# Inverse roots as exp(-0.5 ln) on ScalarE, and other places for the adaLN additions, in a two-layer diffusion step

## What is computed

```python
def rmsnorm(x, g):
    y = xf * lax.rsqrt(jnp.mean(xf * xf, axis=-1, keepdims=True) + NORM_EPS)
    return (y * g).astype(x.dtype)

def modulation(cvec, w, b):                     # adaLN: six vectors of 1024 for each layer
    m = jax.nn.silu(cvec) @ w + b
    return jnp.split(m, 6, axis=-1)

# in each layer l, for each token group:
mix = token_mixer(rmsnorm(x, norm1_g[l]) * (1 + sc1) + sh1, ...)
x = x + gt1 * mix
x = x + gt2 * expert_choice_ffn(rmsnorm(x, norm2_g[l]) * (1 + sc2) + sh2, ...)

# in token_mixer: queries and keys of the 8 attention heads are normed one head at a time
nq = head_rms(na_heads(nq), na_q_g)
nk = head_rms(na_heads(nk), na_k_g)
```

## Time and profile before

| | |
|---|---|
| runs of the kernel before | 3173.14, 3174.12, 3202.10 us (median 3174.12) |
| the profiled execution | 3180.14 us, span of its instructions 3178.4 us |
| granted TensorE clock, mean of the span | 0.956 of 2.4 GHz |
| TensorE matmul busy | 2986.3 us (94% of the span) |
| VectorE busy | 1873.8 us (59%) |
| ScalarE busy | 1359.4 us (43%) |
| GpSimd busy | 546.0 us (17%) |
| HBM | 182 GB/s over the span |

### The profile page before, as it was taken

How to read it: one execution, slowest core, us unless ns; L and a number is a source line. 1 busy time by engine, 2 the same in 40 slices (tenths; PEclk the granted TensorE clock), 3 DMA queues, 4 the chain that set the end, 5 groups by cost and what they waited for, 6 DMA issues and landing times.

```text
span 3178.4 us, 42933 instructions
## 1 busy us (share of the span) xinstructions
PE 2986.3 (94%) x17920; PEld 2452.9 (77%) x17920; DVE 1873.8 (59%) x2079; ACT 1359.4 (43%) x1751; POOL 546.0 (17%) x218
## 2 busy tenths in 40 slices
PE   5999888899997999999989998899999799999998
PEld 3979877799896666767659798799999767666765
DVE  3551743223416888898975436432242488989897
ACT  2143220111106777777751332310110477777775
POOL 2314313132321000000024123143323100000000
PEclk8989899999988999999999899899999899999999
DMA  8613465366433989798994334432443198989896
GB/s 231 82 27 67 89 149 167 110 161 163 112 113 117 343 282 339 280 341 285 338 279 72 41 54 76 91 67 40 80 80 113 53 346 303 328 300 328 301 325 237
DMA packets 357650, 580.80 MB, mean 183 GB/s; under 512 B 13712, under 2 KB 148880, under 8 KB 357328
## 3 DMA queue, kind: packets, MB, share of 16 engines
q1 hardware_dynamic: 297488, 501.26, 54.0%
q10 hardware_dynamic: 51808, 56.53, 5.6%
q0 software_dynamic: 8160, 20.26, 2.0%
HBM read 568.54 MB, written 9.45 MB: 182 GB/s over the span
## 4 chain that ended last, share of the span: by engine, by line
PE 76%; DVE 9%; DMA 7%; DVEq 3%; issue 3%; ACT 2%; ACTq 0%; POOL 0%; SPq 0%; POOLq 0%
PE ps L828 27%; PE ps L1315 8%; PE ps L1318 8%; PE ps L1323 8%; PE ps L792 5%; DMA ring<-w_down 3%; DMA ring<-w_gate 2%; PE ps L1232 2%; PE ps L870 2%; DVE w_lo L2250 2%; DVEq L1976 2%; ACT w_hi L1445 1%; PE ps L1091 1%; PE ps L902 1%; PE ps L1008 1%
## 5 line engine op out<-in xcount | busy, mean ns | idle before, releaser
L2250 DVE TENSOR_TENSOR w_lo<-ring,w_hi 128x2048 fp32r<-128x2048 f32 x256 | 584.1, 2287 | 96.4 <-ACT w_hi L1445 96.1
L828 PE MATMUL ps<-h_hi,w_hi 128*128 128x320 f32 x1792 | 561.6, 313 | 23.6 <-DVE mod L2299 19.4
L828 PE MATMUL ps<-h_lo,w_hi 128*128 128x320 f32 x1792 | 556.7, 311 | 0.0
L828 PE MATMUL ps<-h_hi,w_lo 128*128 128x320 f32 x1792 | 556.5, 311 | 0.0
L1445 ACT ACTIVATE w_hi<-ring 128x2048 fp32r<-128x2048 f32 x256 | 487.1, 1910 | 81.8 <-DMA ring<-w_up 27.2
L668 POOL CAST w_hi<-ring 128x2048 fp32r<-128x2048 f32 (+1 forms) x76 | 143.5, 1888 | 1610.3 <-DMA ring<-w_in 1007.3
L1507 ACT ACTIVATE arena<-ps,par 128x640 f32<-128x640 f32 x88 | 70.0, 796 | 712.5 <-PE ps L828 694.3
L828 PEld LDWEIGHTS ps<-h_hi,w_hi 128*128 128x128 f32 x1792 | 339.3, 189 | 31.5 <-issue 18.9
L670 POOL TENSOR_TENSOR w_lo<-ring,w_hi 128x2048 fp32r<-128x2048 f32 (+1 forms) x76 | 345.0, 4539 | 28.2 <-issue 27.5
L828 PEld LDWEIGHTS ps<-h_lo,w_hi 128*128 128x128 f32 x1792 | 339.3, 189 | 0.5 <-issue 0.5
L828 PEld LDWEIGHTS ps<-h_hi,w_lo 128*128 128x128 f32 x1792 | 339.0, 189 | 0.0
(11 more groups left out here) (311 smaller groups left out, 5446.4 us busy)
## 6 DMA issues: line engine op xcount, KB each, us to landing
ring<-w_gate SPq DMA_DIRECT2D x128, 1024.0 KB, 6.0
ring<-w_up SPq DMA_DIRECT2D x128, 1024.0 KB, 6.5
ring<-w_down SPq DMA_DIRECT2D x128, 1024.0 KB, 6.8
ring<-w_in SPq DMA_DIRECT2D x64, 1024.0 KB, 13.0
arena<-ada_w ACTq DMA_DIRECT2D x40, 1024.0 KB, 5.4
arena<-ada_w SPq DMA_DIRECT2D x8, 1024.0 KB, 15.6
arena<-biasT ACTq DMA_DIRECT2D x16, 512.0 KB, 6.9
ring<-w_o SPq DMA_DIRECT2D x8, 1024.0 KB, 16.3
```

What stands on the lines that cost most here:

```text
L828: last = pe.matmul(ps[:, bank(u) + half, 0:HALF], w[:, k, f0:f0 + P], a[:, k, at], start=(k == 0 and part == 0), stop=(k == KD - 1 and par ...
L2250: dve.tensor_tensor(w_los[g % NW], ring[:, s, :], w_his[g % NW].bitcast(F32), ALU.subtract).then_inc(slot_used[s], 1)
```

## The change

It does three things.

1. Square root and reciprocal become logarithm and exponential, both on ScalarE, in two places: `root_mean` with `root_x`, and `head_roots` with `norm_heads`. In `head_roots` the four logarithms come first, then one drain, then the four exponentials, each of which counts up `root_ready`. (The roots of the mLSTM heads and of the router stay as they are.)
2. In the head of layer 0 the eight first chunks use the banks 0, 4, 0, 4, 0, 2, 4, 6, TensorE turns chunks 4 to 7 right after their rows, waits for other additions than before, and starts the first projection after six additions; VectorE's list has `normed`, `norm_low` and the additions in another order.
3. In the convolution and merge of layer 0 the additions stand elsewhere in VectorE's list: after the product of the unit instead of before the wait for the next one, and chunks 21 and 22 at the end of the convolution instead of behind the first `merge_lows`.

```diff
+        HEAD_BANKS = (0, 4, 0, 4, 0, 2, 4, 6)
         def ada_bank(n):
-            return 4 * (n % 2) if n < ADA_FIRST else bank(U_ADA[n])
+            return HEAD_BANKS[n] if n < ADA_FIRST else bank(U_ADA[n])
...
                     if fresh and j == 0:
                         fresh_units(l, us[0], hi, lo)
+                        if l == 0:
+                            pe.wait_ge(mod_ready, ADA_FIRST)
...
             def ada_first():
                 for n in range(ADA_FIRST):
                     pe.wait_ge(ada_head_landed[n], 16)
-                    if n >= 2:
+                    if 2 <= n < 5:
                         pe.wait_ge(mod_ready, n - 1)
+                    elif n == 5:
+                        pe.wait_ge(*x_root.at(0, 1))
+                    elif n == 6:
+                        pe.wait_ge(mod_ready, 4)
                     ada_rows(n, ada_head[:, n, :].rearrange("p (k n) -> p k n", n=CC))
-                    if n and n != 4:
+                    if n >= 4:
+                        ada_turn(n)
+                    elif n:
                         ada_turn(n - 1)
...
-                ada_turn(ADA_FIRST - 1)
-                pe.wait_ge(mod_ready, ADA_FIRST)
+                pe.wait_ge(mod_ready, 6)
...
             def root_mean(l):
                 act.wait_ge(*x_ss.at(l, 1))
-                act.activation(cols(rstd[:, :]), ps[:, 2:4, 0:HALF], ACT.Sqrt, bias=eps[:, :], scale=1.0 / D)\
-                    .then_inc(x_root.sem, 1)
+                act.activation(cols(rstd[:, :]), ps[:, 2:4, 0:HALF], ACT.Ln, bias=eps[:, :], scale=1.0 / D)
+                act.drain()
+                act.activation(rstd[:, :], rstd[:, :], ACT.Exp, scale=-0.5).then_inc(x_root.sem, 1)
...
             def head_roots(l, u0, tmp, scale):
                 for i in range(KB):
-                    empty(l, u0 + i, tmp[:, i, :], eps[:, :], ACT.Sqrt, scale)
-                    act.drain()
-                    act.sem_inc(root_ready.sem, 1)
+                    empty(l, u0 + i, tmp[:, i, :], eps[:, :], ACT.Ln, scale)
+                act.drain()
+                for i in range(KB):
+                    act.activation(tmp[:, i, :], tmp[:, i, :], ACT.Exp, scale=-0.5).then_inc(root_ready.sem, 1)
...
-                    act.activation(warm[:, :], eps[:, :], ACT.Sqrt)
+                    act.activation(warm[:, :], eps[:, :], ACT.Ln)
...
             def root_x(l):
                 dve.wait_ge(*x_root.at(l, 1))
-                dve.reciprocal(rstd[:, :], rstd[:, :])
                 dve.drain()
...
                     dve.wait_ge(*root_ready.at(l, n0 + i + 1))
-                    dve.reciprocal(tmp[:, i, :], tmp[:, i, :])
-                    dve.drain()
...
# convolution, VectorE
-                        ada_adds(6 * j + 1 if f else max(6 * j - 2, 0), 6 * j + 1 + f)
+                        if f == 0:
+                            ada_adds(max(6 * j - 1, 0), 6 * j + 1)
                         dve.wait_ge(*emptied(l, u_conv(i, 0)))
...
                                                  cols(cc_t[:, i, :]), ALU.add, ALU.mult).then_inc(dve_emptied.sem, 1)
+                        ada_adds(6 * j + 1 + f, 6 * j + 2 + f)
                         dve.drain()
...
                         i = 2 * j + f
-                        ada_adds(6 * j + 2 + f, 6 * j + 3 + f)
                         u = u_conv(i, 2)
...
                             .then_inc(dve_emptied.sem, 1)
+                        ada_adds(6 * j + 3 + f, 6 * j + 4 + f)
...
# merge, VectorE
-                        for n in (ada_of(i - 1),) if i else (*ada_conv(3 * KB - 2), *ada_conv(3 * KB - 1)):
+                        for n in (ada_of(i - 1),) if i else ada_conv(3 * KB - 1):
                             mod_add(n)
...
# head of layer 0, VectorE
-                    for n in range(ADA_FIRST // 2, ADA_FIRST):
-                        mod_add(n)
-                        if n < 6:
-                            normed(l, 2 * n - 4)
-                            normed(l, 2 * n - 3)
-                        norm_low(l, 2 * n - 8)
-                        norm_low(l, 2 * n - 7)
+                    mod_add(4)
+                    normed(l, 4)
+                    mod_add(5)
+                    normed(l, 5)
+                    for k in range(2):
+                        norm_low(l, k)
+                        normed(l, 6 + k)
+                    mod_add(6)
+                    for k in range(2, 4):
+                        norm_low(l, k)
+                    mod_add(7)
+                    for k in range(4, KD):
+                        norm_low(l, k)
```

More of the change, by code:

```diff
@@ L1689, in _ @@
                             norm_high(l, 2 * n - 9)
-                    norm_high(l, KD - 2)
-                    norm_high(l, KD - 1)
+                    for k in range(KD - 2, KD):
+                        norm_high(l, k)
                 else:
```

## The result

| | before | after |
|---|---|---|
| runs shown with the prediction's result | 3173.14, 3174.12, 3202.10, 3179.33 us (median 3176.72) | 3146.58, 3147.25, 3150.19, 3148.21 us (median 3147.73) |
| ratio after to before | | 0.9877, 95% interval 0.9848 to 0.9907 |
| the profiled execution, its span | 3180.14 / 3178.4 us | 3146.58 / 3144.7 us |
| granted TensorE clock, mean | 0.956 | 0.958 |

The ratio is the one on record; the two medians of the few runs shown differ by 29 us, 0.9%. In a later and larger set of runs the kernel before had a median of 3184.06 us (21 runs), and the changed kernel 3145.87 (6 runs): the medians are 38 us apart, and the ratio is 0.9877 again (0.9854 to 0.9901), which is 39 us with an interval of 32 to 46. So the change saves about 1.2%.

What follows compares the result with a forecast made beforehand. TensorE, with matmuls in flight for 94% of the span, was taken to bound the kernel. 5.7 + 5.6 + 5.8 + 23.6 + 2.1 = 42.8 us took 3180.14 to 3137.3, or 3131 against the median 3174.12; range 3119 to 3147.

Steps and rivals of the forecast that it cites:

- Head of layer 0: Start of layer 0: new order and banks let the first projection start near 52.6 instead of 58.33, 5.7 us earlier; bounds 3 and 8.
- Queries and keys: Gap ahead of attention, each layer: attention starts 5.6 us earlier in layer 0, 5.8 in layer 1; bounds 4 and 6.5.
- The late start of the value projection: Keys' roots: a table load delays the first logarithm, which frees a PSUM pair, so the value projection starts about 0.5 us late.
- The store: HBM store that VectorE's value tile 3 waits for: late next, landing 8.5 us after the last norm, at 363.8.
- Convolution and merge: Layer 0, convolution and start of merge: moved additions shorten TensorE's waits and half clock, 23.6 us; bounds 16 and 25.
- CV3: Convolution unit of layer 0 that needs addition 9: gain 3.6 us of waiting and 2.4 of clock, 6.0.
- CV9: Convolution unit of layer 0 that needs addition 17: gain 3.6 us of waiting and 1.4 of clock, 5.0.
- The signs named for this place: Convolution and merge, layer 0: no wait for an addition at CV3 and CV9, one below 1 us at the first gate unit.
- Head of layer 1: Start of layer 1: logarithm and exponential replace root and reciprocal, VectorE scales from 1659.4 instead of 1661.57, 2.1 us; bounds 1 and 2.5.
- One table for both functions: Rival: logarithm and exponential share one table load, as the skill says; 3129 us, chance 0.07.
- the clock in the attention: Effect of the shorter gap on TensorE's clock in attention: taken as 0, with ends +5 and -3 us for each layer.
- The rival in which the clock stays up: At attention the gap shrinks to 1.3 us and the clock stays up: 5 us more for each layer, 3121 us, chance 0.12.
- The rival with the collisions: Convolution: each moved addition behind an odd unit waits for GpSimd's subtraction (4.6 us); sum near 28, 3146 us, chance 0.13.

## Why the prediction came out as it did

The forecast was 0.9864 of before (3131 against 3174.12) and the ratio is 0.9877; in microseconds 3147.73 is 17 above the forecast and 0.7 above the range's top. 10 of these 17 us are the base: three runs gave 3174.12, more than twenty later ones 3184. Worked from the earlier trace rows's own execution the forecast was 3137.3, and that of after took 3146.58.

- *Head of layer 0*, forecast 5.7, measured 7.8. That the root brings next to nothing and the order does it was right (0.9 and 6.5). Undersized was the start: the eight scalings ended at 44.9, not at 46, and the addition behind them at 45.2 instead of 46.4. The chunks' copies then fell between `norm_high`'s earlier than counted: the turn of chunk 6 was at 47.6, not at 49.5.
- *Queries and keys*, forecast 5.6 and 5.8, measured 5.4 and 5.2. The attention starts on its gap of 0.95 and 1.4 us. The two loads for each `head_roots` are there, where the Trainium skill ("ScalarE: Activation LUTs", table sets) has one load for both functions; the rows decide for two. The late start of the value projection was counted; the same load ahead of the query roots, with the second key unit waiting behind it, was not. Hiding both gave 0.9 and 1.0.
- *The store* as what is late next: right. Tile 3's bias, which waits for it, runs at 354.30, 8.3 us behind the last norm (8.5 forecast), and ahead of tile 4's, as forecast.
- *Convolution and merge*, forecast 23.6, measured 22.3. The chunks 21 and 22 were undersized (12.0 forecast, 14.3), the rest oversized (11.6 forecast, 8.0): part of the clock that CV3 and CV9 were to give back went to the first unit, which took 9.9 us in the changed kernel and 7.2 in the profile that the forecast was worked from. The signs named for this place came: a wait of 0.3 us for an addition at CV3, none at CV9, 0.8 at the first gate unit.
- *Head of layer 1*, forecast 2.1: 5.05 less 2.97 is 2.1.
- *One table for both functions*, the rival: the prediction prices it at 2.5 us in one place and at 2.3 in the other. It fell with the two loads, so nothing hangs on it.

The sum at the places is 7.8 + 5.4 + 5.2 + 22.3 + 2.1 = 42.8 us, the 42.8 of the forecast to the digit, and that is luck: the head of layer 0 gave 2.1 more than its term, the others together 2.1 less. As a whole 39 came, with an interval of 32 to 46, so it is not shown that anything is missing. If a step failed, it is the one taken at nothing, the clock in the attention: behind the short gap the attention ran 3 and 1 us longer in the mean, but the rows overlap, and this stays open. The rival in which the clock stays up fell: it takes work in TensorE's gap, a short gap alone doesn't do it. The rival with the collisions was right in its mechanism (4.63 for the second addition of each pair) and wrong in the place: of each pair in the convolution it is the second that is caught, and no wait of TensorE for an addition there is longer than 1.0 us. What it described did happen elsewhere, in the merge, in the kernel before as well.

## What to carry to other kernels

Put a small instruction that another engine waits for right behind the instruction that releases its input, ahead of a chain of tile operations, above all when GpSimd may start a long one at any time. Where TensorE waits a microsecond or two in front of light work, a few matmuls that nobody reads and that fill the wait can be worth as much again as shortening it: here 6.2 and 5.5 us in the two layers, behind 5.4 and 5.2. Before filling a longer wait, look where the half clock lies: in the wait itself it costs nothing. Add up the gains at their places, against several profiles of the same code: one profile pair mixes 40 us of gain with stages that differ by 8 us on their own.

## What the runs showed of the hardware

- The same attention of layer 0, instruction for instruction, took 73.2 to 81.0 us with 16 to 28 us at half clock in five kernels that differ only elsewhere. Filling about 3 us of TensorE's idle time at its start brought the mean to 73.8 us in layer 0 (70.4, 76.3, 75.3, 71.4, 75.6) and 74.5 in layer 1, from 80.0 in both.
- Less time at half clock isn't more speed where TensorE waits anyway: in the router of layer 0 the transposes took the wait's clock from 0.50 to 0.83, the gathers behind it ran at 0.50 as before, and the stage took 115.7 us against 115.6.
- Under GpSimd's subtraction of 128x2048 (4.6 to 5.0 us) VectorE's addition of 128x4, 0.16 us by itself, took up to 4.65, and a cast of 128x640, 0.49 by itself, 4.76.
- In this program a logarithm followed by an exponential costs a table load of 1.28 us each way, every time; loads placed by a dead instruction of 0.20 us in ScalarE's idle time made the stage 0.9 to 1.0 us shorter.
